# The fourth sum of each pair of weight blocks, taken from GpSimd to VectorE

## What is computed

```python
def _swiglu(h, w_gu, w_down):
    g, u = jnp.split(h @ w_gu, 2, axis=-1)
    return (jax.nn.silu(g) * u) @ w_down

def reference(...):
    h = x
    for i in range(DEPTH):
        ...
        h = h + mix.astype(h.dtype)
        h = h + _swiglu(_rmsnorm(h, norm_ffn[i]), ffn_w_gu[i], ffn_w_down[i]).astype(h.dtype)
    return _rmsnorm(h, final_norm)
```

## Time and profile before

| what | value |
|---|---|
| median of 3 runs | 1128.38 us (1128.16 to 1129.77) |
| the profiled execution | 1128.31 us, span 1126.5 us |
| granted TensorE clock | 0.998 of full speed |
| busy | PE 1112.7 us (99%), DVE 884.2 (78%), POOL 596.2 (53%), ACT 540.4 (48%) |
| units of layer 0 | about 208 to 299 us and 360 to 471 us |
| units of layer 1 | about 790 to 881 us and 943 to 1054 us |

### The profile page before, as it was taken

One profiled execution on the slowest core, in us unless ns is written; L12 is line 12 of the kernel. 1 busy time (PEld: TensorE's weight loads), 2 busy tenths in 40 slices (PEclk: granted clock), 3 DMA queues, 4 the chain that ended last, 5 costly groups with the idle time before them and its releaser, 6 DMA issues.

```text
span 1126.5 us, 18571 instructions
## 1 busy us (share of the span) xinstructions
PE 1112.7 (99%) x7114; PEld 1001.3 (89%) x7114; DVE 884.2 (78%) x1309; ACT 540.4 (48%) x1053; POOL 596.2 (53%) x523
## 2 busy tenths in 40 slices
PE   9999999999999999999999999999999999999997
PEld 8877778999988999988998888888999889999886
DVE  6688868999857999777389888769999746899654
ACT  6388834656302555411287777635555103566202
POOL 6467746687215666233156446644875217765241
PEclk9999999999999999999999999999999999999999
DMA  6411125233334333233211001134333344333321
GB/s 197 114 38 38 36 78 149 76 91 105 95 103 112 108 87 108 83 103 94 86 41 41 20 20 38 38 101 123 104 99 90 100 115 113 101 91 98 104 77 75
DMA packets 175399, 98.34 MB, mean 87 GB/s; under 512 B 7880, under 2 KB 171216, under 8 KB 175312
## 3 DMA queue, kind: packets, MB, share of 16 engines
q1 hardware_dynamic: 175296, 97.16, 30.3%
q10 hardware_dynamic: 16, 0.00, 0.0%
HBM read 94.01 MB, written 2.10 MB: 85 GB/s over the span
## 4 chain that ended last, share of the span: by engine, by line
PE 89%; DVE 6%; ACT 2%; issue 2%; POOL 0%; ACTq 0%; DVEq 0%; POOLq 0%
PE bank L1674 21%; PE bank L1678 21%; PE bank L1677 21%; PE bank L2114 14%; PE bank L2387 3%; PE bank L2406 1%; PE bank L2409 1%; PE bank L1904 1%; PE bank L1888 1%; DVE x_lo L3002 1%; DVE w_lo L3002 1%; PE bank L1919 1%; PE bank L1920 1%; PE bank L2318 1%; ACT s_a L1171 0%
## 5 line engine op out<-in xcount | busy, mean ns | idle before, releaser
L1674 PE MATMUL bank<-f_hi,w_lo 128*128 128x512 f32 (+1 forms) x363 | 139.7, 385 | 0.0
L1678 PE MATMUL bank<-f_hi,w_hi 128*128 128x512 f32 (+1 forms) x363 | 139.0, 383 | 0.0
L843 POOL TENSOR_SCALAR w_hi<-raw 128x1408 fp32r<-128x1408 f32 x32 | 44.7, 1396 | 178.1 <-PE bank L1678 150.9
L1677 PE MATMUL bank<-f_lo,w_hi 128*128 128x512 f32 (+1 forms) x363 | 138.9, 383 | 0.0
L1674 PE MATMUL bank<-x_hi,w_lo 128*128 128x256 f32 (+1 forms) x392 | 119.7, 305 | 0.0
L1678 PE MATMUL bank<-x_hi,w_hi 128*128 128x256 f32 (+1 forms) x392 | 118.8, 303 | 0.0
L1677 PE MATMUL bank<-x_lo,w_hi 128*128 128x256 f32 (+1 forms) x392 | 118.7, 303 | 0.0
L857 POOL TENSOR_TENSOR s<-raw 128x512 f32<-128x512 f32 x40 | 70.2, 1754 | 87.6 <-DMA raw<-in_ffn_w_gu 87.6
L1323 ACT ACTIVATE m_u<-bank 128x256 f32<-128x256 f32 x80 | 30.8, 385 | 135.1 <-PE bank L2114 93.8
L2114 PE MATMUL bank<-t_hi,x_lo 128*128 128x256 f32 x320 | 91.2, 285 | 1.1 <-DVE x_lo L3002 1.1
L1674 PE MATMUL bank<-t_hi,g_lo 128*128 128x256 f32 x320 | 90.7, 283 | 0.0
(11 more groups left out here) (390 smaller groups left out, 3664.5 us busy)
## 6 DMA issues: line engine op xcount, KB each, us to landing
raw<-in_ffn_w_gu SPq DMA_DIRECT2D x80, 512.0 KB, 5.2
raw<-in_ffn_w_down SPq DMA_DIRECT2D x32, 704.0 KB, 4.6
w_raw<-in_a_w_qkv SPq DMA_DIRECT2D x10, 512.0 KB, 5.1
w_raw<-in_a_w_o SPq DMA_DIRECT2D x8, 512.0 KB, 4.1
w_raw<-in_ffn_w_gu SPq DMA_DIRECT2D x8, 512.0 KB, 4.0
w_raw<-in_b_w_o SPq DMA_DIRECT2D x8, 512.0 KB, 3.7
w_raw<-in_b_w_in SPq DMA_DIRECT2D x4, 672.0 KB, 4.0
w_raw<-in_b_w_uq SPq DMA_DIRECT2D x4, 576.0 KB, 4.0
```

The costliest lines, as they stand in the source:

```text
L843: pool.tensor_scalar(w_hi[m % 2][:, 0:cols], raw_slot[r % 2][:, 0:cols], 1.0, 1.0, ALU.mult, ALU.mult) \
L1674: first = pe.matmul(o, ll, rh, start=start, stop=False)
L1677: pe.matmul(o, lh, rl, start=False, stop=False)
L1678: return pe.matmul(o, lh, rh, start=False, stop=stop)
```

## The change

The fourth sum is taken out of `more_sums` and becomes a function of DVE, `last_sum`, with the same waits. It is called once for each unit: in the loop behind group 1 of unit j + 1; for unit 2 behind `hidden` of pair 0, ahead of group 1; for unit 3 behind its group 1; and for unit 11 ahead of the last block of the down projection. All 40 units are moved.

```diff
@@ more_sums
-                a12, a22 = (raw_slot[r % 2][:, i * QUART:(i + 1) * QUART] for i in (1, 3))
+                a22 = raw_slot[r % 2][:, 3 * QUART:4 * QUART]
                 pool.wait_ge(s3_ready, u + 1)
                 pool.tensor_tensor(s2, s3, a22, ALU.subtract).then_inc(s2_ready, 1)
-                pool.wait_ge(s2_ready, u + 1)
-                if j == 2:
-                    pool.wait_ge(t_ready, 4 * layer + HK)
-                elif u > 1:
-                    pool.wait_ge(g_ready, 4 * (u - 2) + 4)
-                pool.tensor_tensor(s_last[:, u % 2 * QUART:(u % 2 + 1) * QUART], a12, s2, ALU.add).then_inc(s4_ready, 1)
+            def last_sum(layer, j):
+
+                u, r = unit_of(layer, j), raw_unit(layer, j)
+                dve.wait_ge(s2_ready, u + 1)
+                if j == 2:
+                    dve.wait_ge(t_ready, 4 * layer + HK)
+                elif u > 1:
+                    dve.wait_ge(g_ready, 4 * (u - 2) + 4)
+                dve.tensor_tensor(s_last[:, u % 2 * QUART:(u % 2 + 1) * QUART], raw_slot[r % 2][:, QUART:2 * QUART],
+                                  s_pair[u % 2][:, QUART:2 * QUART], ALU.add).then_inc(s4_ready, 1)
@@ ffn_half, first half
                     hidden(layer, 0)
+                    last_sum(layer, 2)
                     group_lo(layer, 2, 1)
...
                     group_lo(layer, 3, 1)
+                    last_sum(layer, 3)
                     late_gate(layer, 2)
@@ ffn_half, loop over units
                         group_lo(layer, j + 1, 1)
+                        last_sum(layer, j + 1)
@@ ffn_half, down projection
                         group_lo(layer, HALF, 1)
+                        last_sum(layer, HALF)
                     add_down(m, b + 1, h_fin[:, m % 2, :] if final else None)
```

## The result

The changed kernel takes 1133.59 us (1133.09 to 1134.49, 6 runs), the kernel before on the same chip 1127.91 us (1127.24 to 1129.77, 6 runs). The ratio is 1.0043, with a 95% interval from 1.0033 to 1.0053: slower by 0.43%. The profiled execution took 1133.35 us, span 1131.5 us. Predicted were 1133.2 us, with a range of 1129.3 to 1138.5.

The account below looks back on a forecast made before the run. TensorE was taken to bound the kernel, so work moved between POOL and DVE matters only where TensorE waits. From 1128.31 us, +5.72 start, -0.20 unit 3, -1.61 loop waits, +1.00 slip gave 1133.2 us, range 1129.3 to 1138.5.

Parts of the forecast that it names:

- What bounds the kernel: Whole kernel: TensorE busy 1112.7 of 1126.5 us; its waits in the units' stages are about 3 us.
- The price of a turn: Start of units: three rounds of POOL 1.15 us plus DVE 0.28 us make the fourth activation sum 3.04 us later.
- Groups 0 and 1: Unit 2, each layer: TensorE starts group 0 2.32 us late, group 1 2.86 us late in all; 5.72 us for both layers.
- Unit 3: Wait of 0.68 us before group 3: 0.1 us given back per layer, 0.2 us in all.
- The loop: Later units: POOL makes three turns per unit, DVE's round is 10.13 us against TensorE's 10.08, about even.
- The 1.61 us of waits: Loop: TensorE's waits for DVE's low parts, 0.49, 0.37 and 0.75 us, counted as gone.
- The slip: Loop, first half of each layer: some five units lose 0.1 us each with restart, 0.5 us per layer.
- the third rival: Loop: DVE becomes its bound, the round some 10.4 us, 5.4 us more, 1138 to 1140 us; chance 0.13.
- Sum: Whole kernel: 1128.31 + 5.72 - 0.20 - 1.61 + 1.00 = 1133.2 us.
- relief wins: Start of units: POOL's early turns catch no activation sums, or one; faster, about 1125.3 to 1126 us; chance 0.09.
- nothing can be measured: Whole kernel: start costs its low bound or less, unit 3 and loop give all back; +1.0, 1129.3 us; chance 0.12.
- its low bound: Start of units: a POOL turn costs DVE only 0.73 us, about 2.0 us lost per layer.

Follow-up runs that it names:

- the dose: Changed kernel, some of unit 3's POOL sums held for unit 2's group 1: two early turns 1131.13 us, one 1129.15; all held, layer 1 only, 1129.23.
- the repeat: The changed kernel itself, unaltered, run once more on the chip of other follow-ups: 1132.66 us, ratio 1.0038 to the kernel before.
- the hold: Changed kernel, but unit 3's three POOL sums wait until group 1 of unit 2 is done: 1125.75 us, ratio 0.9978.
- the loop alone: Changed kernel with the fourth sums of units 2 and 3 back on POOL, the other 36 on DVE: 1127.88 us, ratio 0.9999.
- the early turns alone: Kernel before, all fourth sums on POOL, unit 2's issued behind unit 3's three sums: 1134.32 us, ratio 1.0061.
- the hold in layer 1 only: Changed kernel, unit 3's POOL sums held until group 1 of unit 2 is done in layer 1 alone: 1129.23 us, ratio 1.0010.

## Why the prediction was right, by its steps

**What bounds the kernel.** Right: the loss is TensorE's waits at the start of each layer's units, and the busy shares did not show it. The prediction counted too few of the waits before, about 3 us. From group 0's first matmul of unit 2 to the last unit, the first halves take 1.38 and 1.91 us more than at the pace of 0.12 us, and layer 0's second half has 0.86: 4.15 us. It left out the waits for group 2 of unit 3 (0.16 and 0.17 us) and the restarts behind the waits.

**The price of a turn.** Predicted were 1.15 us and 0.28 us for each POOL turn and the DVE instruction behind it, 3.04 us in all. Measured: 2.94 us, and 0.96 us a turn by the dose. The rule of the Trainium skill, page "SBUF — State Buffer", section "SBUF: two separate sides", that the lock is held for the whole instruction, would by the prediction's estimate have made it 0.8 us more per layer. That the two engines exclude each other the trace bears out, this size it does not: POOL's instructions of 1.35 us cost 0.96 to 1.0.

**Groups 0 and 1.** TensorE on group 0: predicted 210.07 us, seen 209.94, of which 0.36 us is older than the change; so 1.83 us late in layer 0 and 2.26 in layer 1, where 2.32 was predicted for each. In the other profiles with three turns it was 2.25 to 2.26. The low end of layer 0 is slack: the late f_lo pushed TensorE back 0.36 us while DVE was not. The prediction's step has the slack right (3.04 us of delay, 2.32 at TensorE); its rivals give 0.87 us as the delay that TensorE does not notice, where by that sum it is 0.72. Group 1: predicted 213.56, seen 213.50; its own part 0.54 predicted, 0.61 measured.

**Unit 3.** Predicted 0.1 us given back per layer. In layer 0 its wait fell from 0.68 to 0.53 us, in layer 1 it was gone, which goes with the half clock of the last section; in the repeat the two are 0.33 and 0.63.

**The loop.** The 1.61 us of waits did go: the second half of layer 0 gained 0.66 us against 0.86 predicted, and layer 1's has even periods. DVE's round was predicted at 10.13 us and is 10.17 us. DVE, the same instruction in two successive units, and the moved sum ahead of each:

```profile
251.72 1.78 DVE L3006 TENSOR_TENSOR s_last<-raw,s 128x512 f32<-128x512 f32 x1
253.43 0.41 DVE L3015 TENSOR_TENSOR gate_up<-u_m,bank 128x256 f32<-128x256 f32 x1
...
261.89 1.78 DVE L3006 TENSOR_TENSOR s_last<-raw,s 128x512 f32<-128x512 f32 x1
263.60 0.41 DVE L3015 TENSOR_TENSOR gate_up<-u_m,bank 128x256 f32<-128x256 f32 x1
```

The moved sum takes 1.78 us there, 1.10 of it waiting for POOL, at the median of all forty. The slip was put at 0.5 us for each first half. In layer 1 it is 0.55 us, about 0.1 in each of six units. In layer 0 it is 1.03 us: 0.40 at unit 8, with a wait of 0.32 us at 278.20, and the rest in five others. In layer 0's second half the periods are 10.08 us until the last two, of 10.17 and 10.18 us (449.39 to 459.56 to 469.74): DVE's lead is used up there, as the third rival had it, but only by 0.1 us a unit.

**Sum.** By halves of the layers the prediction has +3.26, -0.86, +2.51 and 0.00 us; measured are +2.75, -0.66, +2.50 and 0.00. The third agrees by luck in part: in it are 1.5 us of half clock, of which the prediction has nothing, and neither group 1's wait (0.54 predicted) nor unit 3's (0.58 was to be left); and 1.1 us of smaller waits and restarts went where 0.75 was counted. In the first, layer 0's longer slip stands against its larger slack.

**The rivals.** That relief wins fell in its premise: POOL's three early turns did catch the three sums. What it would give is close to what the hold gives, since that takes away the early turns alone: 1125.3 to 1126 us was its price, 1125.75 was measured. That nothing can be measured fell with the start, which costs more than its low bound. That DVE becomes the bound of the loop fell with the units' distances, 10.08 to 10.18 us but for one wait at unit 8 of layer 0, and by the loop alone, which costs nothing. The page "GPSIMD Engine Reference", section "Engine selection", of the Trainium skill holds in this case for the instruction (0.68 and 1.29 us) and not for the kernel: with the same forty moves the kernel is 0.43% slower or 0.22% faster, by one wait on POOL.

## What to carry to other kernels

An instruction that waits also holds back those behind it in its queue; when you take it out, ask which of them start earlier and whose ports they take, and give the first of them a wait on the last thing that the bounding engine is short of. Price such a move by what the pair does to each other (here 0.96 us a turn), not by the time of each alone, and look for the stage where the waiting engine has the least slack (0.72 us here). Where turns are unavoidable, as in the loop, moving the instruction a few places may only choose who is hit: in the one such move tried here the time stayed the same.

## What was not expected of the hardware

In layer 1 of the changed kernel TensorE's granted clock fell after the wait for group 0. Windows (length, busy of PE, PEld, DVE, ACT, POOL with counts, granted clock, DMA share, GB/s):

```profile
796.00:799.60 3.60, 3.60 (x20) 3.60 (x19) 3.60 (x5) 2.30 (x5) 0.00 (x0) 0.53 0.04 11
799.60:805.00 5.40, 5.40 (x47) 5.40 (x46) 1.95 (x4) 2.72 (x5) 1.25 (x1) 1.00 0.68 187
```

and matmuls of that stretch:

```profile
796.16 0.42 PE L1668 MATMUL bank<-x_hi,w_lo 128*128 128x256 f32 x1
796.80 0.42 PE L1668 MATMUL bank<-x_hi,w_lo 128*128 128x256 f32 x1
797.44 0.42 PE L1668 MATMUL bank<-x_hi,w_lo 128*128 128x256 f32 x1
```

Every third matmul is shown by this line, so one takes 0.213 us instead of 0.12: the level of 1.2 GHz instead of 2.4, for about 3.4 us from 796.0 us on. In that time 16 matmuls are done, 1.92 us of work at full clock, so 1.5 us are lost. But TensorE, being later, then finds group 1 and unit 3's group 3 ready: from group 0's first matmul to the last piece of the half it is 88.68 us in layer 1, and 88.86 in layer 0, where the clock stayed up and the waits came. Six waits of 2.25 or 2.26 us for group 0 are in the profiles of these kernels (the changed kernel's layer 1, its repeat's two layers, the early turns alone twice, the hold in layer 1 only once); after two of them the clock fell, in the changed kernel's layer 1 and in the repeat's layer 0. After the waits of 1.83 us and less at this place it did not. The window of the repeat:

```profile
209.90:213.30 3.40, 3.40 (x19) 3.40 (x18) 3.40 (x5) 2.53 (x5) 0.00 (x0) 0.50 0.00 0
```

Why two of six, and not the others, stays open; what it costs the whole kernel is below what these runs tell apart.
